# The position bias of the spatial gating: from one-row matmuls on TensorE to an add on VectorE, and a narrower wait before the last product

## What is computed

```python
def spatial_gating(u, v, w_s, b_s):
    n = S // SG_CHUNK                                   # 256 // 128 = 2
    vc = v.reshape(B, n, SG_CHUNK, SG_GROUPS, SG_GROUP_DIM)
    w = jnp.where(causal[None], w_s, 0)
    s = jnp.einsum('gts,bnsge->bntge', w, vc) + b_s.T[None, None, :, :, None]
    return u * s.reshape(B, S, SG_WIDTH)
```

```python
o_attn = _dsa_attention(q, k, v, q_idx, k_idx, w_idx) * jax.nn.silu(z_attn)
mixed = jnp.concatenate([o_attn, o_ssd], axis=-1)
sub = jnp.einsum('bse,ed->bsd', mixed, w_out[layer])
h = _layer_norm(DEEPNORM_ALPHA * h + sub, ln_g[layer], ln_b[layer])
```

## Time and profile before

| | us |
|---|---|
| median of 3 runs | 2175.1 |
| lowest, highest | 2174.7, 2176.28 |
| the profiled execution | 2174.93 |
| its span, first to last instruction | 2173.1 |
| TensorE busy | 2140.2 (98%) |
| VectorE busy | 1269.2 (58%) |
| ScalarE busy | 950.0 (44%) |
| mean granted TensorE clock | 0.991 |

### The profile page before, as it was taken

One profiled execution on the slowest core, in us unless ns is written; L12 is line 12 of the kernel. 1 busy time (PEld: TensorE's weight loads), 2 busy tenths in 40 slices (PEclk: granted clock), 3 DMA queues, 4 the chain that ended last, 5 costly groups with the idle time before them and its releaser, 6 DMA issues.

```text
span 2173.1 us, 32425 instructions
## 1 busy us (share of the span) xinstructions
PE 2140.2 (98%) x14283; PEld 1968.5 (91%) x14283; DVE 1269.2 (58%) x1358; ACT 950.0 (44%) x925; POOL 26.1 (1%) x42
## 2 busy tenths in 40 slices
PE   8999999999999999999999999999999999999996
PEld 6989999878999989989999888999988889988975
DVE  5634465444444566666665544666654667887665
ACT  5433344234443365454444433444443434444543
POOL 2000000000000000000000000000000000000001
PEclk9989999999999999999999999999999999999998
DMA  8535546455556565535555556555566554544462
GB/s 278 191 113 179 171 142 210 159 174 168 181 176 227 192 221 202 172 115 189 175 193 183 177 194 203 175 189 182 174 203 201 168 183 156 175 155 147 144 214 97
DMA packets 243117, 388.38 MB, mean 179 GB/s; under 512 B 14145, under 2 KB 104597, under 8 KB 241825
## 3 DMA queue, kind: packets, MB, share of 16 engines
q1 hardware_dynamic: 240352, 374.50, 52.3%
q0 software_dynamic: 2448, 11.74, 1.5%
q10 hardware_dynamic: 176, 0.07, 0.0%
HBM read 384.19 MB, written 2.10 MB: 178 GB/s over the span
## 4 chain that ended last, share of the span: by engine, by line
PE 97%; DVE 1%; DMA 0%; ACT 0%; issue 0%; SPq 0%; DVEq 0%; ACTq 0%
PE ps L535 92%; PE pm L535 4%; PE pm L538 1%; DVE y L1485 1%; DMA raw<-in_w_in 0%; DVE xx L1493 0%; ACT xth L998 0%; ACT junkB L1018 0%; DVE xtl L1485 0%; DVE wl L1485 0%; SPq L2486 0%; SPq L2479 0%; ACT y L998 0%; DVE bst L2321 0%; DVE y L1493 0%
## 5 line engine op out<-in xcount | busy, mean ns | idle before, releaser
L1485 DVE TENSOR_TENSOR wl<-raw,wh 128x2048 fp32r<-128x2048 f32 (+1 forms) x361 | 806.7, 2243 | 624.4 <-ACT wh L998 624.1
L998 ACT ACTIVATE wh<-raw 128x2048 fp32r<-128x2048 f32 (+1 forms) x361 | 674.2, 1875 | 889.6 <-PE ps L535 886.6
L535 PE MATMUL ps<-xth,wh 128*128 128x256 f32 (+1 forms) x2784 | 791.5, 284 | 1.0 <-DVE xtl L1493 1.0
L535 PE MATMUL ps<-xtl,wh 128*128 128x256 f32 (+1 forms) x2784 | 789.2, 283 | 0.0
L535 PE MATMUL ps<-xth,wl 128*128 128x256 f32 (+1 forms) x2784 | 789.0, 283 | 0.0
L535 PEld LDWEIGHTS ps<-xth,wh 128*128 128x128 f32 (+1 forms) x2784 | 534.2, 192 | 4.7 <-issue 4.1
L535 PEld LDWEIGHTS ps<-xtl,wh 128*128 128x128 f32 (+1 forms) x2784 | 534.3, 192 | 0.5
L535 PEld LDWEIGHTS ps<-xth,wl 128*128 128x128 f32 (+1 forms) x2784 | 534.3, 192 | 0.3
L535 PE MATMUL ps<-wh,xth 128*128 128x512 f32 x800 | 317.2, 396 | 2.1 <-DVE xtl L1485 1.9
L535 PE MATMUL ps<-wh,xtl 128*128 128x512 f32 x800 | 312.4, 390 | 0.0
L535 PE MATMUL ps<-wl,xth 128*128 128x512 f32 x800 | 312.3, 390 | 0.0
(11 more groups left out here) (327 smaller groups left out, 1684.5 us busy)
## 6 DMA issues: line engine op xcount, KB each, us to landing
raw<-in_w_in SPq DMA_DIRECT2D x147, 1024.0 KB, 5.1
raw<-in_ffn_w_up SPq DMA_DIRECT2D x176, 512.0 KB, 4.6
raw<-in_ffn_w_down SPq DMA_DIRECT2D x40, 1024.0 KB, 5.1
raw<-in_w_out SPq DMA_DIRECT2D x32, 1024.0 KB, 5.2
raw<-in_w_proj_b SPq DMA_DIRECT2D x16, 1024.0 KB, 5.2
raw<-in_w_proj_a SPq DMA_DIRECT2D x8, 1024.0 KB, 5.2
raw<-in_xa_wk SPq DMA_DIRECT2D x4, 1024.0 KB, 5.3
raw<-in_xa_wq SPq DMA_DIRECT2D x4, 1024.0 KB, 5.5
```

What stands on the lines that cost most here:

```text
L535: return p.matmul(out, l, r, start=start, stop=stop, skip_group_check=share)
L998: return a.activation(out, in_, func, bias=bias, scale=scale)
L1485: return v.tensor_tensor(out, a, b, op)
```

## The change

The bias tile `sgb` becomes 128x1024: `sg_b` is loaded to all 128 partitions by one DMA (4 KB for each partition) in the same place of GpSimd's queue. TensorE's sixteen one-row matmuls go, and with them its wait for the tables. VectorE now adds the bias to a full bank, as a view that repeats each group's row for both chunks, into `yaf`, waits for that, multiplies `yaf` in place by `uT`, and hands it to ScalarE. In `mix_attn0` both waits become `after("za1") - 1`.

```diff
-    sgb8 = tile("sgb", B + 4, [1, 1024])
+    sgb = tile("sgb", B + 4, [128, 1024])
...
-            p.wait_ge(s_rows, 64)
...
-                        mm(o, vs[:, n, g * 128:(g + 1) * 128], swT[:, g, :], True, False)
-                        t = mm(o, ones[0:1, :], sgb8[0:1, g * 128:(g + 1) * 128], False, True)
+                        t = mm(o, vs[:, n, g * 128:(g + 1) * 128], swT[:, g, :], True, True)
...
-            for i, u in enumerate(use["sg_mix"]):
-                a.wait_ge(u.free_sem, u.free)
+            for i in range(4):
+                heard()
...
-                a.wait_ge(s_used, after("za1"))
+                a.wait_ge(s_used, after("za1") - (i == 0))
...
+            v.wait_ge(s_rows, 64)
...
-                tt(yaf[i % 2], u.ap, flat(uT[:, 2 * i:2 * i + 2, :]), ALU.mult).then_inc(u.free_sem, 1)
+                f4 = yaf[i % 2].rearrange("p (j n t) -> p j n t", j=2, n=2)
+                bias = v3(sgb[:, 256 * i:256 * i + 256], 128).unsqueeze(2)
+                tt(f4, u.ap.rearrange("p (j n t) -> p j n t", j=2, n=2), bc(bias, [128, 2, 2, 128]), ALU.add).then_inc(
+                    u.free_sem, 1)
+                v.wait_ge(u.free_sem, u.free)
+                to_act.add(tt(yaf[i % 2], yaf[i % 2], flat(uT[:, 2 * i:2 * i + 2, :]), ALU.mult))
...
-                v.wait_ge(s_used, after("za1"))
+                v.wait_ge(s_used, after("za1") - (i == 0))
...
-        e.dma_start(sgb8, I["sg_b"][0].rearrange("(o g) t -> o (g t)", o=1)).then_inc(s_rows, 16)
+        e.dma_start(sgb, on_all(I["sg_b"][0].rearrange("g t -> (g t)"))).then_inc(s_rows, 16)
```

## The result

| | before | after |
|---|---|---|
| median, us | 2175.69 (4 runs) | 2154.05 (4 runs) |
| lowest, highest | 2174.7, 2176.58 | 2152.61, 2155.62 |
| profiled execution | 2174.93 | 2154.2 |
| its span | 2173.1 | 2152.4 |

The changed kernel is faster: the ratio is 0.9901, with a 95% interval from 0.9884 to 0.9918. The sign and the two large terms were right. The term for the wider load, the reason given for the clock and the range were not.

The account below looks back on a forecast made before the run. TensorE, busy 2140.2 of 2173.1 us, was taken as the bound. Terms -16.5 - 1.9 + 1.0 = -17.4 us gave 2157.5 against the profiled 2174.9, with 0.2 for the median 2157.7 us; range 2154.5 to 2163.5.

Parts of the forecast that it names:

- the two large terms: TensorE in `sg_mix` with the slow products behind it, 16.5 us less; the wait in `mix_attn0`, 1.9 us less.
- The term for the wider load: At the start: the 512 KB load of `sg_b` delays the last load of unit 0, 1.0 us more (0 to 1.4).
- The pace of `sg_mix`: TensorE in `sg_mix`: 32 instructions at 0.122 us each once the one-row matmuls go, so 18.8 us become 3.9.
- The clock: In `sg_mix`: stays at 1.00, since 3.9 us of such work is less than the 5.7 after which it fell.
- the clock falls all the same: Rival in `sg_mix`: pace 0.122, but the clock falls and products stay slow, giving back 1.6 us; 2159.3 us, chance 0.14.
- the pace stays at 0.21: Rival in `sg_mix`: stage takes 6.7 us, the clock falls and slow products stay; 2162.8 us, chance 0.14.
- The slow tail: TensorE products behind `sg_mix`: 19 matmuls at 0.115 us instead of 0.200, 1.6 us less.
- The wait in `mix_attn0`: Border of `za1` and `w20`: earlier `xth` and `xtl` writes remove TensorE's waits, 1.9 us less.
- the finer wait brings nothing: Rival at `mix_attn0`: the new writes collide with `split_hi` or a late `oaT`; 2159.6 us, chance 0.05.
- VectorE's cover: VectorE in `sg_mix`: four added adds stay hidden before TensorE needs `wl` at `ma1`, 0 us, 0.7 us to spare.
- slower: Case in `sg_mix`: adds far slower than 0.69 us make TensorE stand at `ma1`; 2182 us at 7 us each, chance 0.01.
- no change: Case: adds near 5 us each, or a gain made up for elsewhere on TensorE; chance 0.02.

## Why the prediction was right, and where it was wrong

The forecast as a whole missed: the median, 2154.05, lies 0.45 us below its range. The term that failed is the one for the wider load, +1.0 us in the sum and nothing in the runs. The range failed by leaving no room below for falls of the clock elsewhere in the kernel.

**The pace of `sg_mix` (18.8 to 3.9 us): right, by the right mechanism.** Measured 3.49. The reading of the earlier trace rows, that the first pair behind a product is not slow, was the one that counted. The term was 0.4 us too large because each of rows 7 includes the full length of its last instruction; the steady pace is 0.109 to 0.110. The three kernels with 128 rows, with sorted rows and with 64 rows show that it is the change of height and neither pairing nor the one row, and the weight loads of the sorted kernel show the load that no longer runs ahead. The rule of the Trainium skill that the prediction weighed ("TensorE: Matmul & The Clock Gate", The mechanism), a weight load overlaps only with matmuls on other row groups, would have left the pace near 0.21. The trace does not agree with that line taken alone: full-height matmuls with a new weight block each come at 0.110 us in these kernels, and it is matmuls of unequal height, 64 rows behind 128, that come at 0.207. The same section of the Trainium skill also says that a load into the background weight buffer is pulled ahead, which the prediction left out; with 0.110 us at full height the trace agrees with that.

**The clock (stays at 1.00): right result, wrong reason.** I compared 3.9 us with 5.7. Stages of 7.06, 13.23 and 14.21 us had no fall, and the one with 32 rows had it after 4.1. So the duration was not what decided. What went with the falls was the height of the matmuls between those of 128 rows; by what it acts is open. That the clock stayed at 1.00 was forecast by a comparison that could not have told. The rival *the clock falls all the same* fell. So did a part of the rival *the pace stays at 0.21*, which had the clock fall because its stage would last 6.7 us.

**The slow tail (1.6 us): right.** 17.02 - 15.33 = 1.69 us, with 15.33 the difference of the two stages.

**The wait in `mix_attn0` (1.9 us): right at the border, by luck behind it.** Measured 2.20 to 2.24 in six traces. The first product of `w20` comes 1.76 us sooner, where I had counted 1.6. The idle time of 1.6 runs from the end of the last product (2065.50), but the next product usually starts before that end, 0.12 us behind the last start. The 0.3 that I had placed at unit 1 of `w20` is a wait at 1717.15 that the change leaves as it was; I had read the two pieces of the earlier trace rows as two waits of one place. At unit 1 of `w20` a delay of about the same size did go, 0.26 us at its first product and 0.08 at the next, but no row that I had read gave it. The second product of unit 0 gave another 0.07. The rival *the finer wait brings nothing* fell.

**The load (+1.0): this step failed.** The price was 1.24 us off by the ladder, or about 1.0 if the scatter of the start is left out. I let the bytes of `sgb` begin "near 13.5", 4 us behind their issue as those of the constants had, and let them share with unit 0 for 0.8 us. The overlap is what was wrong: they began near 13.8, most of them moved behind 14.18, and unit 0 landed there, no later than before. Of my three values, the lower end (nothing) was the true one. Whether 1.0 would have been the price of a real overlap is not shown: issued early, the same load cost 1.18 us, but with a wait for `x` in it that I had not thought of, and unit 0 landed only 0.63 later. The prediction's sentence on which queue gets the larger part was right, for what it is worth (64.3 against 40.3% of the engines), but that part was taken from units 1 and 2. The rule of the Trainium skill that the prediction put beside this term ("DMA: Bandwidth & Descriptors", Queues, rings and completion order) would have made it 1.4, further off; since the bytes came too late to meet more than the end of unit 0, no run here tests the rule itself.

**VectorE's cover (0 us, 0.7 to spare): right.** The add took 0.69, as in the earlier trace rows, 0.8 us were left, and the kernel with one more add shows that beyond them it is one for one. The rivals *slower* and *no change* asked for adds of 5 us and more.

**The range: too narrow below.** The sum of the terms was 2.0 us short at its own places (1.24 for the load and the scatter of the start, 0.52 in `sg_mix`, 0.30 at `w20`: 2.06). The other 1.28 us are falls of the clock of 3.4 us each that come and go between executions and that cost up to 1.6 us where they hit dense products: -1.38 near 960 us and +0.10 near 1974. To this comes one that the ladder can't show, since it rests on one trace of before. In that trace the clock was low for 17.1 us in and behind `sg_mix`. In the three other traces that have one-row or 32-row pairs there it was low for 20.5, and the place cost 1.47 to 1.50 us more. So the profiled execution, on which the whole sum was made, was mild at this place, though not as a whole (2174.93 against medians of 2174.65 and 2175.69). The medians are 21.6 us apart, the profiled executions 20.7; that the milder place makes this difference is likely and not shown. My own range allowed 1.6 us for the scatter of three runs and nothing for falls of the clock that the changed kernel may be spared elsewhere, though the earlier trace rows showed what one can cost.

## What to carry to other kernels

Look at the spacing of the starts when a small matmul of another height stands between full ones: a one-row bias costs its pair twice the time at the full clock, and on top it may bring the clock down; give the bias to an engine that has room, or raise it to 128 rows, or at least sort the matmuls by height (that brought the pace back, but the clock still fell). Before work is laid on another engine, count from its last stage to the next tile that TensorE needs; work behind a wait lengthens the chain in full, and whether it hides ahead of one was not measured here. A line of waits with a total and a count does not say where they are: look each one up in the timeline before it goes into a sum. A sum made against one trace should say how often the clock falls in it and what each fall costs, and take that into the range.

## What the runs showed of the hardware that I had not expected

- fp32 matmuls of 128 columns, each behind a weight load of its own: 0.110 us for an instruction where all have 128 rows, about 0.13 where heights change every eight instructions, 0.207 where 128 rows alternate with 64 rows at the full clock, 0.21 with 1 row. Between equal heights the weight load starts 0.12 us ahead of its matmul, at a change of height together with it (122.67 and 122.68).
- The granted clock fell to 0.50 with 1 or 32 rows between the 128 (4.1 to 5.6 us into the stage, low for 17.1 to 20.5 us; 10.2 us where the heights were sorted) and stayed at 1.00 with 64 (13.2 us) and with 128 alone (14.2 us).
- A load of 512 KB on GpSimd's queue, issued at 9.53 us among others, landed 7.1 us later; it cost nothing there. Issued first, it made the first product 1.2 us later, with ScalarE waiting 1.37 us for `x`.
- Falls of the clock of 3.4 us come in some executions and not in others, between 936 and 961 us in and behind a stretch with short standstills of TensorE, near 1940 or 1974 us under a TensorE that was busy throughout, and make up to 1.6 us of difference each between runs of one kernel.
